# Second block, first mixer: where the forget gate's sums stand, and the head statistics

## The chip, the cores and the metric

The kernel runs on one core of one Trainium2 chip. The metric is the time of one launch on the device, in microseconds, smaller is better. The engines named are TensorE (matmuls), VectorE and ScalarE (which read its results out of PSUM, a memory of eight banks) and SyncE, which issues the weight transfers.

## The reference

The program computes two small networks one after the other on 256 tokens of width 1024, in float32. The first (attention, a pooling mixer, two mixtures of experts) ends with a norm; the second takes its result. The change lies in the second one's first mixer, `mixer_ab`, which has two branches: an mLSTM with four heads and an S5 state space model.

```
proj = x @ w_in;  xm, zm, us = the three thirds of proj
xc = silu(causal_dwconv(xm));  q, k from xc, v from xm (blocks of 4)
gates = concat(q, k, v) @ w_if + b_if            # per token: 4 input, 4 forget gates
b = cumsum(log_sigmoid(forget));  a = input - b;  m = running max of a
h = mLSTM(q, k, v) with weights exp(b_t - b_s + i_s - m_t), causal
hn = (h - mean(h)) * rsqrt(var(h) + EPS) * mh_gain      # per head and token
out_m = (hn + skip * xc) * silu(zm)
y = gelu(s5_ssm(us));  out_s = y * sigmoid(y @ w_glu + b_glu)
result = concat(out_m, out_s) @ w_out
```

The reference does the mLSTM in chunks of 64; the kernel does all 256 tokens at once, which needs the sums b and the running maximum m over the whole sequence before the heads' weights can be formed.

## The kernel before

Each stage of the program (`stage`, `run_stages`) hands one list of work to each engine, and no engine starts a stage before all have ended the one before. Within a stage every engine works through its own list strictly in the order written, and the lists meet at semaphores. The order around this change is therefore written by hand, in `all_pe`, `all_act` and `all_dve` of `mixer_ab`. `v(...)` makes VectorE wait for its own last instruction.

The pieces that the change touches:

- Tiles. TensorE's `project` (L1941) computes 128 output channels for all 256 tokens in eight matmuls (16 records in the trace). Tiles are numbered: US 0 to 3, XM 4 to 7, QKV 8 to 19, VT 20 and 21, GATES 22, and the gate branch's Z, 23 to 26. They rotate through banks 4, 5 and 6 of `ps`. ScalarE takes each tile out and counts `tile_taken`; `open_tile` waits for that count. The Z tiles are taken with Silu.
- The S5 branch runs in four pieces c. `states(c)` (L1951) makes the inputs of the state in banks 0 to 3; VectorE does `turn_in(c, 0..3)` (L2127), `turned_in(c)` (L2133, L2134), `scans(c)` (L2139, L2140, eight scans), `turn_out(c)` (L2146 to L2149); TensorE does `outputs(c)` (L1960) into bank 7, and VectorE `take_y(c)` (L2153). All pieces use the same buffers, so turn_in(c + 1) waits for outputs(c), and outputs(c) for turn_out(c).
- The forget gate. VectorE's `forget` (L2172 to L2175), two activations on ScalarE, VectorE's `log_forget` (L2179, counts `lf_ready`); TensorE's sums, three tiny matmuls with a triangle (L2038 to L2040, count `b_ready`); VectorE's `sums` (L2183, L2184, count `a_ready`); two transposes (L2043, `aT_ready`); VectorE's `running_max` (L2188 to L2191, `m_ready`); two transposes back (L2048, `mT_ready`); VectorE's `floor` (L2195). Before, the sums and the transposes of a come behind all four Z tiles, and use banks 4 and 5.
- The heads. `scores(h)` (L1971 to L1977), exponentials on ScalarE, `weigh(h)` (L2202), `mix(h)` (L1985 to L1987), `finish(h)` (L2210 to L2215), which writes `h_tok` and counts `num_taken`.
- The end. `skip` (L2240) makes skip * xc. `statistics` (L2222 bn_stats, L2226 bn_aggr, L2228 the variance plus EPS, `var_ready`); a square root on ScalarE; `normed` (L2232, L2235, `hn_ready`); eight transposes (L2066, `hnT_ready`); `mlstm_out` (L2246, L2248). Beside it the S5 branch: Gelu on ScalarE after the fourth take_y (L2105, `g_done`), TensorE's `glu(n)` (L1991), a sigmoid on ScalarE (L2110), `glu_out(n)` (L2252). ScalarE does Gelu first, then the square root, then the sigmoids.

Then the stage ends, and `project_out` (L1789) multiplies by w_out. Its weights are loaded while the mixer runs. The weights of the feed-forward behind it are asked for by SyncE when the stage has ended, because part of the weight ring serves as scratch space in this stage.

Of the kernel before, what the change touches and what calls it, by code (L numbers as in the profile page):

```python
# [20 lines left out]
P = 128  # L21
D = 1024
S = 256
TT = S // P
# [129 lines left out]
def build_program(nc, A, out):  # L154

    with ExitStack() as ctx:
# [1720 lines left out]
        def mixer_ab():  # L1877
# [50 lines left out]
            def bank(n):  # L1928

                return ps[:, 4 + n % 3, :]  # L1930

            def all_pe(pe):
                def open_tile(n):
                    if n >= 3:
                        pe.wait_ge(tile_taken, n - 2)
                    return bank(n)
# [90 lines left out]
                ins.then_inc(tile_ready, 1)  # L2027
                outputs(1)
                w = ring.take(pe, ("ab_in", 1))
                for j in range(4):  # L2030
                    project(w, j, Z + j)
                    if j == 1:
                        states(3)
                release(pe)

                pe.wait_ge(tile_taken, Z + 4)
                pe.wait_ge(lf_ready, 1)
                pe.matmul(ps[:, 4, 0:4], const("upto"), t1[:, 0, :], start=True, stop=True)  # L2038
                pe.matmul(ps[:, 4, 4:8], ones, t1[:, 0, :], start=True, stop=False)
                pe.matmul(ps[:, 4, 4:8], const("upto"), t1[:, 1, :], start=False, stop=True).then_inc(b_ready, 1)  # L2040
                pe.wait_ge(a_ready, 1)
                for t in range(TT):
                    ins = pe.transpose(ps[0:4, 5, t * P:(t + 1) * P], a_tok[:, t, :], ident)  # L2043
                ins.then_inc(aT_ready, 1)
                outputs(2)
# [3 lines left out]
                ins.then_inc(mT_ready, 1)  # L2049

                scores(0)
# [11 lines left out]
                pe.wait_ge(hn_ready, 8)  # L2063
                for h in range(4):
                    for t in range(TT):
                        ins = pe.transpose(ps[:, 4 + h // 2, (h % 2) * S + t * P:(h % 2) * S + (t + 1) * P], h_tok[:, t, h, :], ident)  # L2066
                ins.then_inc(hnT_ready, 1)
# [44 lines left out]
            def all_dve(dve):  # L2112
# [68 lines left out]
                def sums():  # L2181
                    dve.wait_ge(b_ready, 1)
                    v(dve.tensor_copy(b_tok, ps[:, 4, 0:8].rearrange("p (t h) -> p t h", t=TT)))  # L2183
                    dve.tensor_tensor(a_tok, pre[:, :, 0:4], b_tok, ALU.subtract).then_inc(a_ready, 1)  # L2184

                def running_max():
                    dve.wait_ge(aT_ready, 1)
                    v(dve.tensor_copy(a_rows[0:4, :], ps[0:4, 5, 0:S]))  # L2188
                    v(dve.tensor_tensor_scan(m_rows[0:4, :], ones[0:4, 0:1].to_broadcast([4, S]), a_rows[0:4, :], 0.0,
                                             ALU.mult, ALU.max))  # L2190
                    dve.tensor_scalar(m_rows[0:4, :], m_rows[0:4, :], -1.0, None, ALU.mult).then_inc(m_ready, 1)  # L2191
# [26 lines left out]
                def statistics():  # L2218
                    dve.wait_ge(num_taken, 4)
                    for t in range(TT):  # L2220
                        for h in range(4):
                            ins = dve.bn_stats(stats[:, t, h, :], h_tok[:, t, h, :])  # L2222
                    v(ins)
                    for t in range(TT):
                        for h in range(4):
                            ins = dve.bn_aggr(mean_var[:, t, h, :], stats[:, t, h, :])  # L2226
                    v(ins)
                    dve.tensor_scalar(sd, mean_var[:, :, :, 1], EPS, None, ALU.add).then_inc(var_ready, 1)  # L2228

                def normed():  # L2230
                    dve.wait_ge(sd_ready, 1)
                    v(dve.reciprocal(rstd, sd))  # L2232
                    for t in range(TT):
                        for h in range(4):
                            dve.tensor_scalar(h_tok[:, t, h, :], h_tok[:, t, h, :], mean_var[:, t, h, 0:1], rstd[:, t, h:h + 1],  # L2235
                                              ALU.subtract, ALU.mult).then_inc(hn_ready, 1)
# [6 lines left out]
                def mlstm_out():  # L2243
                    dve.wait_ge(hnT_ready, 1)
                    for h in range(4):
                        v(dve.scalar_tensor_tensor(out=conv[:, h, :], in0=ps[:, 4 + h // 2, (h % 2) * S:(h % 2 + 1) * S],  # L2246
                                                   scalar=col("ab_mh_gain_2", h), in1=conv[:, h, :], op0=ALU.mult, op1=ALU.add))
                        dve.tensor_tensor(mixT[:, h, :], conv[:, h, :], szT[:, h, :], ALU.mult)  # L2248
# [29 lines left out]
                forget()  # L2278
                take_y(1)
# [3 lines left out]
                turned_in(2)  # L2283
                scans(2, range(4))
                sums()
                turn_out(2)
                running_max()
                take_y(2)
                for i in range(4):
                    turn_in(3, i)  # L2290
                    if i == 0:
                        floor()
# [11 lines left out]
                skip()  # L2304
                finish(3)
                take_y(3)
                statistics()
# [381 lines left out]
```

## Time and profile before

| | |
|---|---|
| median of 3 runs | 2192.69 us (2184.86 to 2197.79) |
| the profiled execution, its own time | 2188.47 us |
| its span | 2186.4 us, 22473 instructions |
| TensorE matmul busy | 1731.5 us (79%) |
| VectorE busy | 501.8 us (23%) |
| ScalarE busy | 218.1 us (10%) |
| the mixer of this change | 1336 to 1454 us of the span |

The span is the profiled execution from its first to its last instruction; its own time holds what lies around the span, too. Times in the views are microseconds from the span's start. A timeline row has the start, the length, the engine, the line of the code, the operation with its output and inputs and the number of instructions merged in it, and in brackets how long the engine was idle before it and what ended that. Buffers carved out of one large tile are all called arena, hT, xn, gates or ring_buffer. PEclk is the granted clock of TensorE: 1.00 is 2.4 GHz, 0.50 is 1.2 GHz, and a value between them is a mean over the slice.

### The profile page before, as it was taken

Reading aid. Unit: us, or ns where it says so; the run is one execution under the profiler, and the core shown is the slowest. Engines: PE = TensorE matmul, PEld = TensorE weight load, DVE = VectorE, ACT = ScalarE, POOL = GpSimd, SP = SyncE. Lnnn points to the kernel's source line nnn. Section 1 sums busy time; section 2 is a strip of 40 time slices with the busy share of each in tenths; the row PEclk is TensorE's granted clock in tenths of the full one; section 3 lists DMA queues with packets and bytes.
Section 4 is the critical chain, followed back from the end, with each engine's and each line's share of the span. In section 5 each row is a group of like instructions: output and inputs, shape, how many; then the busy total and the mean of one; then the engine's idle time right before and its main releaser. Section 6 shows DMA issues by size and latency. Waiting matters only on the chain. (4 is left out here: it accounts for less than half of the span.)

```text
span 2186.4 us, 22473 instructions
## 1 busy us (share of the span) xinstructions
PE 1731.5 (79%) x9018; PEld 1000.1 (46%) x9019; DVE 501.8 (23%) x1168; ACT 218.1 (10%) x510; POOL 97.9 (4%) x125
## 2 busy tenths in 40 slices
PE   5999978866666576776666657878999899889998
PEld 3755553322222253232222215646885486558853
DVE  1213362111101125411111016861000203420001
ACT  1001020000000020000000001321000212110000
POOL 1010010000000007500000000000000000000000
PEclk9999968978877867898787778889999899899999
DMA  9969249999999956799999994133335434124330
GB/s 363 385 234 406 93 181 402 421 422 422 422 422 422 409 233 250 322 406 421 422 422 422 422 408 158 39 140 122 142 107 210 164 116 154 39 87 154 116 135 19
DMA packets 122665, 581.10 MB, mean 266 GB/s; under 512 B 10820, under 2 KB 15272, under 8 KB 67160
## 3 DMA queue, kind: packets, MB, share of 16 engines
q1 hardware_dynamic: 120416, 573.90, 65.4%
q0 software_dynamic: 1104, 2.86, 0.4%
q10 hardware_dynamic: 1064, 3.17, 0.4%
q8 instruction: 60, 0.98, 0.2%
q14 instruction: 21, 0.17, 0.0%
HBM read 578.86 MB, written 1.05 MB: 265 GB/s over the span
## 5 line engine op out<-in xcount | busy, mean ns | idle before, releaser
L1306 PE MATMUL ps<-ring_buffer,arena 128*32 128x512 f32 x2048 | 309.6, 763 | 170.6 <-DMA ring_buffer<-in_exp_w 167.9
L1831 PE MATMUL ps<-hT,ring_buffer 128*128 128x256 f32 x1408 | 309.9, 382 | 4.1 <-issue 2.6
L1831 PEld LDWEIGHTS ps<-hT,ring_buffer 128*128 128x128 f32 x1408 | 268.7, 192 | 45.2 <-issue 6.3
L1306 PEld LDWEIGHTS ps<-ring_buffer,arena 128*32 128x32 f32 x2048 | 82.1, 135 | 384.8 <-issue 325.0
L1331 PE MATMUL ps<-ring_buffer,arena 128*32 128x512 f32 x1088 | 155.8, 725 | 100.3 <-DMA ring_buffer<-in_exp_w 89.3
L1839 PE MATMUL ps<-ring_buffer,arena 128*128 128x512 f32 x352 | 154.2, 595 | 3.0 <-DVE arena L1872 1.9
L1331 PEld LDWEIGHTS ps<-ring_buffer,arena 128*32 128x32 f32 x1088 | 41.0, 130 | 204.3 <-issue 191.6
L1496 DVE TENSOR_TENSOR arena<-arena,ps 128x512 f32<-128x512 f32 x18 | 19.2, 1065 | 411.6 <-PE ps L1306 411.6
L1839 PEld LDWEIGHTS ps<-ring_buffer,arena 128*128 128x128 f32 x352 | 65.9, 190 | 90.4 <-issue 87.8
L1276 PE MATMUL ps<-arena,xn 128*128 128x128 f32 x640 | 82.0, 289 | 12.9 <-DVE arena L1466 12.9
L1276 PEld LDWEIGHTS ps<-arena,xn 128*128 128x128 f32 x640 | 78.6, 203 | 28.1 <-issue 22.3
L2364 PE MATMUL ps<-hT,ring_buffer 128*128 128x256 f32 x384 | 87.1, 389 | 1.9 <-issue 1.0
L1872 DVE TENSOR_TENSOR arena<-arena,ps 128x256 f32<-128x256 f32 x44 | 18.5, 421 | 295.9 <-ACT arena L1866 295.9
L2364 PEld LDWEIGHTS ps<-hT,ring_buffer 128*128 128x128 f32 x384 | 74.4, 195 | 15.0 <-issue 3.5
L1419 ACT ACTIVATE arena<-ps,mod,gain 128x128 f32<-128x128 f32 x72 | 27.1, 457 | 419.0 <-PE ps L1276 419.0
L1789 PE MATMUL ps<-ring_buffer,hT 128*128 128x512 f32 x128 | 59.7, 627 | 3.3 <-DVEq L237 3.0
L715 PE MATMUL ps<-hT,ring_buffer 128*128 128x256 f32 x256 | 58.6, 391 | 3.2 <-ACTq L237 2.5
L1512 DVE TENSOR_TENSOR arena<-ps,gates 128x512 f32<-128x512 f32 x16 | 11.1, 692 | 211.8 <-PE ps L1331 211.8
L1345 PE MATMUL ps<-arena 128*128 128x512 f32 x128 | 59.3, 605 | 0.0
L499 PE MATMUL ps<-ring_buffer,arena 128*32 128x512 f32 x384 | 50.0, 642 | 9.2 <-DMA ring_buffer<-in_ada_w 8.3
L715 PEld LDWEIGHTS ps<-hT,ring_buffer 128*128 128x128 f32 x256 | 50.0, 197 | 13.0 <-issue 3.4
L1436 ACT ACTIVATE arena<-ps 128x512 f32<-128x512 f32 x18 | 10.8, 597 | 416.7 <-PE ps L1306 416.7
(501 smaller groups left out, 1565.5 us busy)
## 6 DMA issues: line engine op xcount, KB each, us to landing
ring_buffer<-in_exp_w SPq DMA_DIRECT2D x384, 1024.0 KB, 18.6
ring_buffer<-in_ffn_w SPq DMA_DIRECT2D x30, 2048.0 KB, 7.9
ring_buffer<-in_ada_w SPq DMA_DIRECT2D x24, 2048.0 KB, 12.6
ring_buffer<-in_c_w_in SPq DMA_DIRECT2D x8, 2048.0 KB, 7.8
ring_buffer<-in_attn_w_in SPq DMA_DIRECT2D x6, 2048.0 KB, 17.0
ring_buffer<-in_ab_w_in SPq DMA_DIRECT2D x3, 2048.0 KB, 19.8
ring_buffer<-in_ffn_w SPq DMA_DIRECT2D x6, 1024.0 KB, 7.8
ring_buffer<-in_attn_w_o SPq DMA_DIRECT2D x2, 2048.0 KB, 12.8
```

The source lines that it names most:

```text
L499: pe.matmul(ps[g * WIDE:(g + 1) * WIDE, COND, :], spread_c[:, 2 * pair + k, row:row + WIDE], w[:, k, 512 * n:512 * (n + 1)], start=(first ...
L715: ins = pe.matmul(ps[:, n % BANKS, 0:S], w[:, k, j * P:(j + 1) * P], hT[:, k, :], start=(k == 0), stop=(k == KD - 1))
L1276: ins = pe.matmul(ps[:, BXA + k // 4, (k % 4) * P:(k % 4 + 1) * P], xn[:, t, k * P:(k + 1) * P], pick[:, t, :], start=(t == 0), stop=(t == ...
L1306: ins = pe.matmul(ps[c, bank, :], tokens[:, 4 * phase + k, c], halves[j][:, k, :], start=(phase == 0 and k == 0), stop=(phase == 1 and k = ...
L1331: ins = pe.matmul(ps[c, bank, :], tokens[:, 2 * phase + k, c], halves[j][:, k, half * 512:(half + 1) * 512], start=(phase == 0 and k == 0) ...
L1345: ins = pe.matmul(ps[:, 2 * half + t, :], weights[:, t, :], values[:, half * 512:(half + 1) * 512], start=opens, stop=False, skip_group_ch ...
L1419: return eng.activation(o, src, ACT.Identity, scale=G[:, k:k + 1], bias=H[:, k:k + 1])
L1496: dve.tensor_tensor(to.rearrange("c (h k p) -> c h p k", h=2, k=2), gated.rearrange("c (h p k) -> c h p k", h=2, k=2), ps[:, bank, :].rear ...
L1789: ins = pe.matmul(ps[:, 2 * c + t, :], fT[:, k, t * P:(t + 1) * P], w[:, k, :], start=(k == 0), stop=(k == KD - 1))
L1831: ins = pe.matmul(ps[:, f % 8, i * S:(i + 1) * S], w[:, k, j * P:(j + 1) * P], hT[:, k, :], start=(k == 0), stop=(k == KD - 1))
L1839: ins = pe.matmul(ps[:, 2 * half + t, :], aT[:, r + k, t * P:(t + 1) * P], w[:, k, 512 * half:512 * half + 512], start=(r + k == 0), stop= ...
L2364: ins = pe.matmul(ps[:, n % 8, 0:S], w[:, k, j * P:(j + 1) * P], hT[:, k, :], start=(k == 0), stop=(k == KD - 1))
```

## The change

The sums, the transposes of a and of m all use bank 6, and the Z tiles rotate through banks 4 and 5 only. TensorE's order becomes: gates, Z0, outputs(1), Z1, the sums, Z2, the transposes of a, states(3), Z3, the transposes of m, outputs(2), scores. In VectorE's list sums moves ahead of scans(2), running_max ahead of turn_out(2), floor ahead of take_y(2), and skip ahead of take_y(1). The statistics are done for one head at a time: those of heads 0 to 2 between finish(2) and finish(3), that of head 3 and the variance (now `variances`) between finish(3) and take_y(3). `normed` goes head by head, the transposes of two heads are signalled as soon as they are done, and mlstm_out waits for each half. The number of computing instructions stays the same.

```diff
             def bank(n):
-                return ps[:, 4 + n % 3, :]
+
+                return ps[:, 4 + n % 3, :] if n < Z else ps[:, 4 + (n - Z) % 2, :]
             def all_pe(pe):
                 def open_tile(n):
-                    if n >= 3:
+                    if n >= Z:
+                        pe.wait_ge(tile_taken, n - 1)
+                    elif n >= 3:
                         pe.wait_ge(tile_taken, n - 2)
                     return bank(n)
@@ -2025,29 +2028,29 @@
                         ins = pe.matmul(o[:, 8 * t:8 * t + 8], qkvT[:, n, t * P:(t + 1) * P], w_if[:, n, :],
                                         start=(n == 0), stop=(n == 11))
                 ins.then_inc(tile_ready, 1)
+                w = ring.take(pe, ("ab_in", 1))
+                project(w, 0, Z)
                 outputs(1)
-                w = ring.take(pe, ("ab_in", 1))
-                for j in range(4):
-                    project(w, j, Z + j)
-                    if j == 1:
-                        states(3)
-                release(pe)
-
-                pe.wait_ge(tile_taken, Z + 4)
+                project(w, 1, Z + 1)
                 pe.wait_ge(lf_ready, 1)
-                pe.matmul(ps[:, 4, 0:4], const("upto"), t1[:, 0, :], start=True, stop=True)
-                pe.matmul(ps[:, 4, 4:8], ones, t1[:, 0, :], start=True, stop=False)
-                pe.matmul(ps[:, 4, 4:8], const("upto"), t1[:, 1, :], start=False, stop=True).then_inc(b_ready, 1)
+                pe.matmul(ps[:, 6, 0:4], const("upto"), t1[:, 0, :], start=True, stop=True)
+                pe.matmul(ps[:, 6, 4:8], ones, t1[:, 0, :], start=True, stop=False)
+                pe.matmul(ps[:, 6, 4:8], const("upto"), t1[:, 1, :], start=False, stop=True).then_inc(b_ready, 1)
+                project(w, 2, Z + 2)
                 pe.wait_ge(a_ready, 1)
                 for t in range(TT):
-                    ins = pe.transpose(ps[0:4, 5, t * P:(t + 1) * P], a_tok[:, t, :], ident)
+                    ins = pe.transpose(ps[0:4, 6, t * P:(t + 1) * P], a_tok[:, t, :], ident)
                 ins.then_inc(aT_ready, 1)
-                outputs(2)
+                states(3)
+                project(w, 3, Z + 3)
+                release(pe)
                 pe.wait_ge(m_ready, 1)
                 for t in range(TT):
                     ins = pe.transpose(ps[:, 6, t * P:(t + 1) * P], m_rows[:, t * P:(t + 1) * P], ident)
                 ins.then_inc(mT_ready, 1)
-
+                outputs(2)
+
+                pe.wait_ge(tile_taken, Z + 4)
                 scores(0)
                 for h in range(4):
                     if h < 3:
@@ -2060,11 +2063,12 @@
                 pe.wait_ge(g_done, 1)
                 for n in range(3):
                     glu(n, w)
-                pe.wait_ge(hn_ready, 8)
                 for h in range(4):
+                    pe.wait_ge(hn_ready, 2 * h + 2)
                     for t in range(TT):
                         ins = pe.transpose(ps[:, 4 + h // 2, (h % 2) * S + t * P:(h % 2) * S + (t + 1) * P], h_tok[:, t, h, :], ident)
-                ins.then_inc(hnT_ready, 1)
+                    if h % 2:
+                        ins.then_inc(hnT_ready, 1)
                 glu(3, w)
                 release(pe)
@@ -2180,12 +2184,12 @@
                 def sums():
                     dve.wait_ge(b_ready, 1)
-                    v(dve.tensor_copy(b_tok, ps[:, 4, 0:8].rearrange("p (t h) -> p t h", t=TT)))
+                    v(dve.tensor_copy(b_tok, ps[:, 6, 0:8].rearrange("p (t h) -> p t h", t=TT)))
                     dve.tensor_tensor(a_tok, pre[:, :, 0:4], b_tok, ALU.subtract).then_inc(a_ready, 1)
                 def running_max():
                     dve.wait_ge(aT_ready, 1)
-                    v(dve.tensor_copy(a_rows[0:4, :], ps[0:4, 5, 0:S]))
+                    v(dve.tensor_copy(a_rows[0:4, :], ps[0:4, 6, 0:S]))
                     v(dve.tensor_tensor_scan(m_rows[0:4, :], ones[0:4, 0:1].to_broadcast([4, S]), a_rows[0:4, :], 0.0,
                                              ALU.mult, ALU.max))
                     dve.tensor_scalar(m_rows[0:4, :], m_rows[0:4, :], -1.0, None, ALU.mult).then_inc(m_ready, 1)
@@ -2215,23 +2219,23 @@
                         ins = dve.tensor_scalar(h_tok[:, t, h, :], o[:, t, 0:M_DIM], r[:, t:t + 1], None, ALU.mult)
                     ins.then_inc(num_taken, 1)
-                def statistics():
-                    dve.wait_ge(num_taken, 4)
+                def statistics(h):
+                    dve.wait_ge(num_taken, h + 1)
                     for t in range(TT):
-                        for h in range(4):
-                            ins = dve.bn_stats(stats[:, t, h, :], h_tok[:, t, h, :])
+                        ins = dve.bn_stats(stats[:, t, h, :], h_tok[:, t, h, :])
                     v(ins)
                     for t in range(TT):
-                        for h in range(4):
-                            ins = dve.bn_aggr(mean_var[:, t, h, :], stats[:, t, h, :])
+                        ins = dve.bn_aggr(mean_var[:, t, h, :], stats[:, t, h, :])
                     v(ins)
+
+                def variances():
                     dve.tensor_scalar(sd, mean_var[:, :, :, 1], EPS, None, ALU.add).then_inc(var_ready, 1)
                 def normed():
                     dve.wait_ge(sd_ready, 1)
                     v(dve.reciprocal(rstd, sd))
-                    for t in range(TT):
-                        for h in range(4):
+                    for h in range(4):
+                        for t in range(TT):
                             dve.tensor_scalar(h_tok[:, t, h, :], h_tok[:, t, h, :], mean_var[:, t, h, 0:1], rstd[:, t, h:h + 1],
                                               ALU.subtract, ALU.mult).then_inc(hn_ready, 1)
@@ -2241,8 +2245,8 @@
                     v(ins)
                 def mlstm_out():
-                    dve.wait_ge(hnT_ready, 1)
                     for h in range(4):
+                        dve.wait_ge(hnT_ready, h // 2 + 1)
                         v(dve.scalar_tensor_tensor(out=conv[:, h, :], in0=ps[:, 4 + h // 2, (h % 2) * S:(h % 2 + 1) * S],
                                                    scalar=col("ab_mh_gain_2", h), in1=conv[:, h, :], op0=ALU.mult, op1=ALU.add))
                         dve.tensor_tensor(mixT[:, h, :], conv[:, h, :], szT[:, h, :], ALU.mult)
@@ -2276,20 +2280,20 @@
                 scans(1, range(4))
                 turn_out(1)
                 forget()
+                skip()
                 take_y(1)
                 log_forget()
                 for i in range(4):
                     turn_in(2, i)
                 turned_in(2)
+                sums()
                 scans(2, range(4))
-                sums()
+                running_max()
                 turn_out(2)
-                running_max()
+                floor()
                 take_y(2)
                 for i in range(4):
                     turn_in(3, i)
-                    if i == 0:
-                        floor()
                 turned_in(3)
                 weigh(0)
                 scans(3, range(2))
@@ -2301,10 +2305,12 @@
                 turn_out(3)
                 weigh(3)
                 finish(2)
-                skip()
+                for h in range(3):
+                    statistics(h)
                 finish(3)
+                statistics(3)
+                variances()
                 take_y(3)
-                statistics()
                 normed()
                 for n in range(3):
                     glu_out(n)
```

## Rows read from the trace of the kernel before

**Rows 1.** Busy time by stretch: stretch, length, then each engine's busy time (instructions).
```profile
core 0: us, PE busy (x) PEld busy (x) DVE busy (x) ACT busy (x) POOL busy (x), PEclk, DMA share, GB/s
1336.00:1454.00 118.00, 96.46 (x596) 77.21 (x594) 96.61 (x180) 29.35 (x55) 0.00 (x0) 0.90 0.11 41
```

**Rows 2.** Waits of VectorE, 1336 to 1455: total, times, longest.
```profile
DVE xn L2153 <- PE ps L1960: 6.0, 3, 2.8
DVE arena L2183 <- PE ps L2040: 4.3, 1, 4.3
```

**Rows 3.** Timeline of TensorE at the mixer's end.
```profile
1438.07 0.80 PE L1985 MATMUL ps<-arena,hT 128*128 128x129 f32 x2 [5.50 <-DVE hT L2202]
...
1444.29 5.42 PE L1991 MATMUL ps<-xn,ring_buffer 128*128 128x256 f32 x24 [1.79 <-ACT xn L2105]
...
1454.55 29.80 PE L1789 MATMUL ps<-ring_buffer,hT 128*128 128x512 f32 x64 [2.24 <-DVEq L237]
```

**Rows 4.** Timeline of TensorE, 1368 to 1413.
```profile
1368.16 1.07 PE L1960 MATMUL ps<-ring_buffer,arena 128*32 128x256 f32 x16
...
1369.48 0.62 PE L1960 MATMUL ps<-gates,arena 128*32 128x256 f32 x8
...
1387.52 1.93 PE L1960 MATMUL ps<-ring_buffer,arena 128*32 128x256 f32 x16 [0.32 <-DVE gates L2149]
...
1390.75 7.17 PE L1941 MATMUL ps<-hT,ring_buffer 128*128 128x256 f32 x32
...
1412.62 1.93 PE L1960 MATMUL ps<-ring_buffer,arena 128*32 128x256 f32 x16 [4.28 <-DVE gates L2149]
```

**Rows 5.** Timeline of VectorE, 1390 to 1417.
```profile
1390.97 0.48 DVE L2153 SCALAR_TENSOR_TENSOR xn<-arena,cols,ps 128x256 f32<-128x256 f32 x1 [2.84 <-PE ps L1960]
...
1391.44 2.35 DVE L2127 TENSOR_TENSOR ring_buffer<-ps,arena 128x1024 f32<-128x1024 f32 x2
...
1407.54 0.17 DVE L2183 COPY arena<-ps 128x8 f32<-128x8 f32 x1 [4.29 <-PE ps L2040]
...
1407.82 1.22 DVE L2146 TENSOR_TENSOR ring_buffer<-xn,arena 128x1024 f32<-128x1024 f32 x1
...
1412.49 0.41 DVE L2188 COPY ring_buffer<-ps 4x256 f32<-4x256 f32 x1
...
1416.34 0.48 DVE L2153 SCALAR_TENSOR_TENSOR xn<-arena,cols,ps 128x256 f32<-128x256 f32 x1 [2.42 <-PE ps L1960]
```

**Rows 6.** Granted clock of TensorE in slices of 1 us.
```profile
1390.00:1391.00 1.00, 1.00 (x13) 0.83 0.00 0
1410.00:1411.00 1.00, 0.00 (x0) 0.91 0.00 0
1434.00:1435.00 1.00, 0.00 (x0) 0.86 0.00 0
1441.00:1442.00 1.00, 1.00 (x20) 0.73 0.02 8
```

**Rows 7.** Timeline of VectorE at the mixer's end.
```profile
1439.24 1.13 DVE L2240 TENSOR_SCALAR arena<-arena,cols 128x256 f32<-128x256 f32 x4
1440.41 0.16 DVE L2210 COPY small<-ps 128x2 f32<-128x2 f32 x1
...
1442.57 0.48 DVE L2153 SCALAR_TENSOR_TENSOR xn<-arena,cols,ps 128x256 f32<-128x256 f32 x1 [0.77 <-PE ps L1960]
1442.97 1.64 DVE L2222 BATCH_NORM_STATS2 arena<-ring_buffer 128x6 f32<-128x128 f32 x8
1444.64 0.64 DVE L2226 BATCH_NORM_AGGREGATE arena<-arena 128x2 f32<-128x6 f32 x8
...
1445.77 0.20 DVE L2232 RECIPROCAL arena<-arena 128x8 f32<-128x8 f32 x1 [0.28 <-ACT arena L2107]
```

**Rows 8.** Groups by line, VectorE: count, busy us, mean ns of one, idle before.
```profile
L2222 DVE BATCH_NORM_STATS2 arena<-ring_buffer 128x6 f32<-128x128 f32 x8 | 1.6, 278 | 0.0
```

**Rows 9.** Timeline of ScalarE: Gelu.
```profile
1443.09 1.06 ACT L2105 ACTIVATE xn<-xn 128x1024 f32<-128x1024 f32 x1 [10.93 <-DVE xn L2153]
```

## The prediction

> **What bounds the kernel now.** I read the busy time by stretches first. The kernel takes 2186.4 us of span, but the changed lines all lie in one stretch of 118 us, in which VectorE is busy for 96.61 us and TensorE for 96.46 [rows 1]. Busy shares don't say which of two equally busy engines leads, so the waits of VectorE in that stretch come next: 4.3 us once at the forget gate's sums (L2183), and 6.0 us in three pieces at take_y (L2153) [rows 2]. The timelines give the order. Between these waits VectorE is gapless to the last instruction of the stage, while TensorE waits for it again and again: 4.28 us ahead of outputs(2), 5.50 ahead of mix(3) [rows 3, 4]. The stage ends when VectorE does, and the output projection (L1789) starts 2.24 us after TensorE's last work, released by VectorE's queue [rows 3]. So the price of this change is what it does to VectorE's chain between 1387 and 1454 us. The stages before are untouched. The stages after have their weights long before they need them: the output projection begins at once when released, and the weight stream of the feed-forward starts only when the whole stage is done. They are shifted and nothing else.
>
> **Edit A: one gate tile (Z0) before outputs(1).** In the kernel before, outputs(1) starts on TensorE at 1387.52, 0.32 us behind the gates' matmuls (done at 1387.2), and ends at 1390.75, 3.23 us; take_y(1) runs on VectorE at 1390.97 after 2.84 us idle [rows 4, 5]. Now project(Z0) stands ahead of it in the same queue. Two projections take 7.17 us at the full clock, one 3.58 [rows 4]. But here the granted clock is at its lower level, 1.2 GHz, until about 1390.5 (the slice 1390:1391 shows 0.83, the mean of both levels) [rows 6]. So 3.3 us of Z0 pass at half speed and do 1.65 us of its work, and 1.93 follow at full speed: Z0 ends at 1392.45. outputs(1) then runs at the full clock, as outputs(0) did: 1368.16 to 1369.48 + 0.62, that is 1.94 us [rows 4]. It ends at 1394.4, and take_y(1) starts at 1394.55, which is 3.6 us later than before. Nothing else can be done by VectorE in that time except skip() (1440.41 - 1439.24 = 1.17 us [rows 7]), which is moved into this gap and so costs nothing here. Bounds: 1.9 us if the clock is full from the start of Z0, 7.0 if it is low throughout (7.17 + 3.3). I take 3.6, the value at the clock of these rows.
>
> **Edit B: sums and maximum between the tiles, in bank 6.** The sums' matmuls no longer stand behind the fourth Z tile, but behind the second: Z1 ends at 1394.4 + 3.58 = 1398.0, the forget gate's logarithm comes right behind take_y(1) (1395.0), so this added wait holds nothing, and b is ready at about 1398.8. VectorE wants it after turn_in(2) and turned_in(2), at 1402.1: no wait. The 4.29 us of idle before L2183 go [rows 2, 5]. On TensorE Z2 (to 1402.4), the transposes of a, states(3) (eight small products, about 1 us) and Z3 follow, to 1407.7. The wait for a holds Z3 by 0.1 us; states(3) is about 5 us later than before, but turn_in(3) wants it at 1417 only. What is late next: running_max now stands ahead of turn_out(2) instead of behind it. Before, its 1.43 us (1412.49 to 1413.92) lay in the time in which VectorE waited for outputs(2); now they are on the chain [rows 5]. From take_y(1) to take_y(2) the chain is now: take_y and log_forget 0.47, turn_in(2) to the last scan(2) 11.81 (1391.44 to 1407.54 - 4.29), sums 0.28, running_max 1.43, turn_out(2) 4.67 (1407.82 to 1412.49), and outputs(2) with its handovers 3.85 (1412.49 to 1416.34, TensorE again at the lower level after 4 us of waiting) [rows 4, 5]. That is 22.51 against 25.37 before: 2.9 us gained. With edit A's 3.6 take_y(2) comes 0.7 us later than before; floor(), taken out of turn_in(3), returns 0.07. So VectorE is 0.6 us late when turn_in(3) is done, and up to finish(2) nothing in that part is reordered, on either engine; TensorE's scores and mixes follow VectorE there, and move with it.
> Bounds for B: a gain of 4.3 us if running_max were hidden after all, and of 1.5 if outputs(2) were delayed by its place behind the maximum's transposes.
>
> **Edit C: statistics head by head, skip() away.** Before, finish(2) was done at 1439.24, then skip() 1.17, finish(3) from 1440.41 to 1441.80, 0.77 us of waiting for outputs(3), and take_y(3) at 1442.57 [rows 7]. Now three statistics stand between, and the fourth and variances() ahead of take_y(3). All eight bn_stats took 1.64 us in a row, 0.205 each, but one alone lasts 0.278; all eight bn_aggr took 0.64 [rows 7, 8]. Head by head each pair is closed by a wait for its own end: 0.205 + 0.278 + 0.03 for two bn_stats, 0.23 + 0.04 for two bn_aggr, together 0.8 us a head, 3.2 for four against 2.35 in one piece. So: 1439.24 + 0.6 (late) + 2.4 + 1.4 (finish(3)) + 0.8 + 0.25 (a wait for finish(3), variances) = 1444.7 for take_y(3), against 1442.57: 2.1 us later. What was behind take_y(3) on VectorE is now ahead of it, but take_y(3) leads the longer branch: Gelu on ScalarE follows it at once (1443.09), and the square root, whose result VectorE takes at 1445.77, stands behind Gelu and a table load in ScalarE's own queue [rows 7, 9]. The reciprocal therefore comes 3.1 to 3.2 us behind take_y(3) either way, and statistics that were free inside these microseconds are now paid.
> The Trainium skill, "VectorE: DVE Perf Modes", section on the drain, has it that eight copies take the same time with a semaphore after each as with one at the end. By it the four heads would cost 2.35 us and take_y(3) would come 0.85 us earlier. The row of 0.205 each against 0.278 alone speaks for my value, since these overlap when nothing is waited for [rows 7, 8].
>
> **The tail.** glu(0) to glu(2) start when Gelu is done and took 5.42 us at the full clock [rows 3]. mlstm_out waits behind glu_out(2), so for these; that the head transposes signal in two halves gives nothing, since the first half is done only when glu_out(2) is anyway. But TensorE has now been idle for longer before glu: outputs(3) ends 0.6 us later, Gelu 2.1 later, so the gap of 1.79 us becomes 3.3 [rows 3]. After the work that ended at 1408.3 (4.28 us before outputs(2)) the clock fell within the slice 1410:1411, 2.6 us later; after 1432.6 (5.50 us before mix(3)) within 1434:1435 [rows 6]. Once work is back it takes about 3.4 us at the lower level (mix(3) at 1438.07 to slice 1441:1442) [rows 6]. So glu runs for about 3.3 us at half speed, which costs 1.65.
> The Trainium skill, "TensorE: Matmul & The Clock Gate", section "What's actually happening", says that the clock follows how busy the engine has been lately; by that rule a longer gap speaks against this change. The trace agrees in its two falls.
> Bounds for this term: 0 (the gap of 1.79 us left the clock at its upper level) and 2.7 (all of glu at half speed until it is half as long again).
>
> **Sum.** +3.6 - 2.9 - 0.1 + 1.5 + 1.65 = +3.7 us. The profiled execution took 2188.47 us, so 2192.2 by it. That execution is 4.2 us under the median of the runs shown, 2192.69; against the median it is 2196.4, which I take as 2196.
>
> **Rivals.**
> 1. *The clock doesn't bite.* Z0 runs at full speed from its start (-1.7), the gap before glu leaves the clock up (-1.65), and the split statistics cost what they did in one piece (-0.85): -0.5 us, 2192. For it: the gap of 1.79 us stayed at the upper level. Against: at the place of Z0 the trace shows the lower level for certain.
> 2. *The idle times really come out of the chain.* 4.3 us before the sums, 0.8 before take_y(3) and skip's 1.2 go, and only running_max's 1.4 is paid: -4.9, 2188. For it: these are the waits of VectorE that the profile shows. It needs outputs(1) not to be later, and TensorE's queue is in order, so there is little for it.
> 3. *The other side: TensorE becomes the bound while it turns the Z tiles.* If the clock stays at its lower level from 1387 us on, each of the four tiles takes 7.17 us instead of 3.58. Z0 to Z3, outputs(1), states(3) and the small products then last some 36 us and outputs(2) ends 11 us later than before; with the 3 us of the last part that is +14, 2207. It decides from the point where Z3 ends after turn_out(2), 1413 us. Against it: before, the clock was up again 3.3 us after work came, and the new order has TensorE busier there.
> 4. *Nothing that a chain shows*: the change is in effect neutral (+-2 us), as errors of my terms cancel.
>
> **Chances.** The forecast (+2 to +6) 55%; rivals 1 and 4 together 27%; rival 2 10%; rival 3 3%; 5% for what I don't see. All but rival 3 are below the 0.5%, 11 us, that a measurement of this kernel can tell from no change: its three runs lie 13 us apart. That spread, more than the mechanisms, sets the range: 2187 (rival 2, near the lowest run) to 2204. Faster by over 0.5%: 3%. Within: 92%. Slower: 5%.
>
> **What would show it.** In the trace after: take_y(1) 3 to 4 us later than 1390.97 (a wait of about 5 us before it, with skip ahead of it); no wait before the copy of the sums; take_y(2) within a microsecond of 1416.3; statistics of a head 0.8 us; take_y(3) near 1444.7; the granted clock at 0.5 when glu begins; the output projection starting near 1458 instead of 1454.55. I am wrong if take_y(1) is not late, if VectorE waits anywhere between take_y(1) and turn_out(2), or if the output projection starts before 1454.

## The result, and the profile after

The changed kernel takes 2192.23 us (median of 20 runs, 2178.86 to 2205.87). With 17 more runs beside it, the kernel before has a median of 2180.27 over 20 runs; its first three alone, known ahead, had 2192.69. The ratio is 1.0048, interval 1.0028 to 1.0067: slower by about 10.5 us (the two medians are 12.0 us apart), just inside the 0.5% that the prediction counts as no change. The prediction had 2196 us and +3.7. Of all runs of the experiments below, one, of the fourth, took 5801.83 us, where the eleven others of its kernel took 2169 to 2190 us; it is left out of the ratio.

The page of the changed kernel, its own time 2191.72 us, has the same amount of work (two instructions more in the record); the last row is the granted clock in tenths, in 40 slices of the span:

```profile
span 2189.9 us, 22475 instructions
PE 1729.5 (79%) x9018; PEld 1001.6 (46%) x9019; DVE 501.7 (23%) x1168; ACT 218.2 (10%) x510; POOL 98.0 (4%) x125
...
PEclk9999988978887778988887888889999899599999
```

**In the mixer** the chain went as predicted. The absolute times are about 9.8 us earlier than those of the kernel before, because the untouched stages ahead of the mixer were shorter in this execution; so intervals are compared. VectorE's timeline answers to [rows 5, 7], with L2157 for take_y, L2244 skip, L2187 the copy of the sums, L2192 running_max, L2225 bn_stats:

```profile
1378.26 1.14 DVE L2244 TENSOR_SCALAR arena<-arena,cols 128x256 f32<-128x256 f32 x4
1384.57 0.48 DVE L2157 SCALAR_TENSOR_TENSOR xn<-arena,cols,ps 128x256 f32<-128x256 f32 x1 [5.17 <-PE ps L1963]
...
1392.09 0.17 DVE L2187 COPY arena<-ps 128x8 f32<-128x8 f32 x1
...
1397.16 0.41 DVE L2192 COPY ring_buffer<-ps 4x256 f32<-4x256 f32 x1
...
1407.03 0.48 DVE L2157 SCALAR_TENSOR_TENSOR xn<-arena,cols,ps 128x256 f32<-128x256 f32 x1 [3.69 <-PE ps L1963]
...
1429.85 0.47 DVE L2225 BATCH_NORM_STATS2 arena<-ring_buffer 128x6 f32<-128x128 f32 x2
1430.36 0.25 DVE L2228 BATCH_NORM_AGGREGATE arena<-arena 128x2 f32<-128x6 f32 x2
1430.64 0.49 DVE L2225 BATCH_NORM_STATS2 arena<-ring_buffer 128x6 f32<-128x128 f32 x2
...
1434.74 0.47 DVE L2157 SCALAR_TENSOR_TENSOR xn<-arena,cols,ps 128x256 f32<-128x256 f32 x1
...
1437.85 0.20 DVE L2236 RECIPROCAL arena<-arena 128x8 f32<-128x8 f32 x1 [2.64 <-ACT arena L2111]
```

The copy of the sums has no wait any more (4.29 us before), skip lies in front of the wait of 5.17 us for outputs(1), and nothing stands idle before the last take_y. Each head's statistics take 0.79 us. TensorE's timeline answers to [rows 3, 4]; L1944 is project, L1963 outputs, L1994 glu:

```profile
1377.11 5.46 PE L1944 MATMUL ps<-hT,ring_buffer 128*128 128x256 f32 x16
1382.50 1.07 PE L1963 MATMUL ps<-ring_buffer,arena 128*32 128x256 f32 x16
...
1436.44 8.22 PE L1994 MATMUL ps<-xn,ring_buffer 128*128 128x256 f32 x24 [3.47 <-ACT xn L2109]
...
1449.48 0.70 PE L1789 MATMUL ps<-ring_buffer,hT 128*128 128x512 f32 x1 [2.21 <-DVEq L237]
```

Z0 took 5.46 us, since it began at the lower clock; glu(0) to glu(2) took 8.22 us instead of 5.42. The granted clock in slices of 1 us shows why: the gap before glu is now 3.47 us long and the clock falls in it.

```profile
1435.00:1436.00 1.00, 0.00 (x0) 0.65 0.00 0
1436.00:1437.00 1.00, 0.56 (x1) 0.50 0.00 0
...
1441.00:1442.00 1.00, 1.00 (x4) 0.50 0.00 0
1442.00:1443.00 1.00, 1.00 (x6) 0.94 0.00 0
```

**Behind the mixer** is what the prediction did not have: the heads of the second mixer, `mixer_c`, whose code and inputs are untouched. Before, these 192 matmul records took 39.0 us from their first to the next output projection, now 50.6. Slices of 5 us from the start of the heads, in the kernel before:

```profile
1862.61:1867.61 5.00, 3.75 (x29) 1.00 0.91 345
1867.61:1872.61 5.00, 5.00 (x24) 0.56 0.00 0
1872.61:1877.61 5.00, 5.00 (x31) 0.76 0.00 0
1877.61:1882.61 5.00, 4.97 (x37) 1.00 0.00 0
```

and in the changed one:

```profile
1856.24:1861.24 5.00, 3.75 (x29) 1.00 0.88 336
1861.24:1866.24 5.00, 5.00 (x24) 0.57 0.02 3
1866.24:1871.24 5.00, 5.00 (x23) 0.50 0.00 0
1871.24:1876.24 5.00, 5.00 (x22) 0.50 0.00 0
...
1891.24:1896.24 5.00, 5.00 (x20) 0.50 0.00 0
```

In both the clock falls between 5.5 and 6 us into the heads. Before, it rises again 12.4 us in; now it stays at 1.2 GHz to the end, and TensorE does 20 to 24 records in 5 us instead of 37. On the page of the changed kernel it is the one digit 5 in the row PEclk, the 35th of 40 slices.

So the spans differ like this: mixer from outputs(0) to the output projection +4.7; the output projection behind it -1.7 (29.8 to 28.1 us, since the clock no longer falls in it); the feed-forward between +0.4; the heads +11.6; the output projection behind these -2.1 (30.15 to 28.1, since it now starts at the upper clock); what follows +0.4; and what lies ahead of outputs(0) -9.8. Sum +3.5, which is 2189.9 - 2186.4. Without the last term the two executions are 13.3 us apart, which lies inside the interval of the ratio (6 to 15 us). That term is no effect of the change: over all executions traced below the mixer begins between 1322.7 and 1341.6 us, with the same code ahead of it.

### The profile page after: what moved, and what is told of

The parts are those of the page before. It is cut to its first block and busy times, and to the rows that moved or that the text cites. A ratio compares the mean times of both kernels' runs of the same rounds, so it can differ in the third digit from the quotient of the medians.

```text
span 2189.9 us, 22475 instructions
## 1 busy us (share of the span) xinstructions
PE 1729.5 (79%) x9018; PEld 1001.6 (46%) x9019; DVE 501.7 (23%) x1168; ACT 218.2 (10%) x510; POOL 98.0 (4%) x125
## 5 line engine op out<-in xcount | busy, mean ns | idle before, releaser
L1306 PE MATMUL ps<-ring_buffer,arena 128*32 128x512 f32 x2048 | 305.0, 753 | 172.3 <-DMA ring_buffer<-in_exp_w 169.6
L1331 PE MATMUL ps<-ring_buffer,arena 128*32 128x512 f32 x1088 | 155.5, 724 | 102.4 <-DMA ring_buffer<-in_exp_w 92.2
L1276 PEld LDWEIGHTS ps<-arena,xn 128*128 128x128 f32 x640 | 79.2, 205 | 27.2 <-issue 21.5
L499 PE MATMUL ps<-ring_buffer,arena 128*32 128x512 f32 x384 | 49.3, 633 | 9.0 <-DMA ring_buffer<-in_ada_w 8.1
```

Source lines behind the costliest of these rows:

```text
L499: pe.matmul(ps[g * WIDE:(g + 1) * WIDE, COND, :], spread_c[:, 2 * pair + k, row:row + WIDE], w[:, k, 512 * n:512 * (n + 1)], start=(first ...
L1276: ins = pe.matmul(ps[:, BXA + k // 4, (k % 4) * P:(k % 4 + 1) * P], xn[:, t, k * P:(k + 1) * P], pick[:, t, :], start=(t == 0), stop=(t == ...
L1306: ins = pe.matmul(ps[c, bank, :], tokens[:, 4 * phase + k, c], halves[j][:, k, :], start=(phase == 0 and k == 0), stop=(phase == 1 and k = ...
L1331: ins = pe.matmul(ps[c, bank, :], tokens[:, 2 * phase + k, c], halves[j][:, k, half * 512:(half + 1) * 512], start=(phase == 0 and k == 0) ...
```

## Experiments

All times in us. "Mixer" runs from outputs(0) to the output projection, "heads" from the first matmul of mixer_c's heads to its output projection, each from the one profiled execution; the ratio is that of the timed runs to the kernel before. (The first expectations measure the mixer from its first project. Those first tiles passed at the lower clock in some executions, 33.2 to 33.4 us to outputs(0) instead of 31.1, ahead of everything that was changed; so I compare from outputs(0).)

| kernel | to take_y(1) | to take_y(2) | to take_y(3) | glu to projection | mixer | heads | ratio (95%) |
|---|---|---|---|---|---|---|---|
| before | 22.8 | 25.4 | 26.2 | 10.3 | 86.4 | 39.0 | 1 |
| changed | 26.2 | 22.5 | 27.7 | 13.0 | 91.1 | 50.6 | 1.0048 (1.0028-1.0067) |
| 1 outputs(1) first | 23.0 | 21.5 | 27.7 | 11.8 | 85.7 | 41.4 | 1.0041 (1.0020-1.0061) |
| 2 statistics whole | 26.2 | 22.5 | 26.1 | 10.2 | 86.7 | 39.0 | 1.0010 (0.9987-1.0033) |
| 3 both undone | 22.8 | 21.6 | 26.4 | 10.2 | 82.8 | 39.0 | 0.9981 (0.9962-1.0000) |
| 4 and maximum late | 22.8 | 19.5 | 27.0 | 10.2 | 81.3 | 39.0 | 0.9990 (0.9965-1.0016) |
| 5 before again | 22.8 | 25.4 | 26.3 | 10.3 | 86.4 | 39.0 | 1.0000 (0.9981-1.0019) |
| 6 only the split | 22.8 | 25.4 | 27.6 | 13.3 | 90.8 | 50.5 | 1.0067 (1.0040-1.0094) |
| 7 before, heads filled | 22.9 | 25.4 | 26.3 | 10.3 | 86.5 | 36.2 | 0.9983 (0.9964-1.0002) |
| 8 changed, heads filled | 26.2 | 22.5 | 27.7 | 13.0 | 91.1 | 36.2 | 1.0002 (0.9982-1.0021) |
| 9 changed, glu filled | 26.2 | 22.5 | 27.7 | 10.2 | 88.3 | 39.0 | 1.0000 (0.9975-1.0026) |
| 10 before, shifted | 22.8 | 25.4 | 26.2 | 14.1 | 90.2 | 41.4 | 1.0026 (1.0004-1.0047) |
| 11 changed again | 26.2 | 22.5 | 27.7 | 13.1 | 91.1 | 50.6 | 1.0036 (1.0008-1.0064) |
| 12 as 4, heads filled | 22.8 | 19.5 | 27.0 | 10.2 | 81.3 | 36.2 | 0.9955 (0.9934-0.9976) |

**Experiments 1 to 4: the parts of the change.**

```diff
 # 1
+                outputs(1)
                 project(w, 0, Z)
-                outputs(1)
 # 2: statistics() in one piece as before
-                for h in range(3):
-                    statistics(h)
                 finish(3)
-                statistics(3)
-                variances()
                 take_y(3)
+                statistics()
+                variances()
 # 3: 1 and 2;  # 4: 3, and
-                running_max()
                 turn_out(2)
-                floor()
+                running_max()
 # with floor() in turn_in(3), and outputs(2) ahead of the transposes of m
```

> The changed kernel with outputs(1) ahead of project(Z0) again; all else as changed. Measured in the trace by the mixer's length (first project of the mixer to the first matmul of the output projection: 117.5 us before, 122.2 changed). Theory 1 (the added us in the mixer are VectorE's chain, 3.4 of them by the gate tile ahead of outputs(1)): take_y(1) comes 3.4 us earlier, nothing new is waited for, mixer 118.8, or 117.5 if outputs(2), which then waits for a shorter time, keeps the full clock. Rival (TensorE's order does not matter, the clock sets it): mixer stays within 1 us of 122.2. For the whole program two theories on the other 7 us that the 20 timed runs show beyond the mixer: theory D (a draw: the heads of mixer_c, 38 us at 2.4 GHz and 50 at 1.2, fall into either by chance, whatever this change does): totals of this kernel lie in two groups some 10 us apart, as those of before and changed do, with its share of slow ones anywhere. Theory P (the change shifts mixer_c against something, which makes its heads slow): this kernel, 3 us shorter, has a share of slow ones different from the changed one and no one kernel has both in plenty.

> The changed kernel with the statistics in one piece behind take_y(3), as before; skip stays early, Z0 stays ahead of outputs(1). Theory 1 (the split puts the statistics ahead of take_y(3), and by it Gelu, the square root and glu, which then starts at the lower clock): take_y(3) 1.5 us earlier than changed, the wait before glu back at 1.8 us, glu(0) to glu(2) 5.4 us instead of 8.2, mixer 122.2 - 1.5 - 2.8 = 117.9 us. If glu's lower clock had nothing to do with the gap: 120.7. Rival (the statistics are hidden either way): 122.2. Theory D or P for the whole as in the first run.

> Both undone: of the change only the sums and the maximum between the tiles in bank 6, and skip in the wait for outputs(1). Theory 1: 2.9 us of the idle before the sums are gained and nothing is paid, mixer 114.5 us, against 117.5 before; ratio to before 0.9987 by the chain alone. Rival (the terms do not add, TensorE becomes the bound): mixer 116 or more. Theory D: the total may still lie up to 7 us off that on either side, by the share of slow runs.

> As the third, and running_max behind turn_out(2) again, with outputs(2) ahead of the maximum's transposes: the maximum lies in VectorE's wait for outputs(2). Theory 1: another 1.4 us, and outputs(2) waits for 1 us instead of 4, so it keeps the full clock and is 1.3 us shorter: mixer 111.8 to 113.1 us. Rival: the transposes of the maximum, now behind outputs(2), delay scores(0) and weigh(0): mixer 114.5 or more.

In the mixer theory 1 holds in all four, with larger gains than expected in the first and the third. Putting outputs(1) first brings 5.4 us: 3.2 at take_y(1), 1.0 because outputs(2) begins after a shorter wait and partly at the upper clock, 1.2 in glu. Leaving the statistics whole brings 4.4: 1.6 at take_y(3) and 2.8 in glu. Of the third kernel's 3.6 us gain, 3.7 lie between take_y(1) and take_y(2). The fourth gains 2.1 more there and gives 0.7 back by take_y(3). VectorE's waits at take_y(2) and take_y(3) in the fourth kernel:

```profile
1402.78 0.48 DVE L2157 SCALAR_TENSOR_TENSOR xn<-arena,cols,ps 128x256 f32<-128x256 f32 x1 [0.70 <-PE ps L1963]
...
1429.80 0.48 DVE L2157 SCALAR_TENSOR_TENSOR xn<-arena,cols,ps 128x256 f32<-128x256 f32 x1 [2.21 <-PE ps L1963]
```

The totals tell something else: the first kernel, whose mixer is 0.7 us shorter than before, is 9 us slower. The two slow kernels, 1 and the changed one, are those with split statistics, and they have the longer heads. (The first kernel's profiled execution, 2180.14 us, was one of its fastest; its median is 2187.5. So its 41.4 us may understate what its heads take as a rule; one profiled execution can't tell.)

**Experiments 5 and 6: is the slow head stage a draw?** The fifth is the kernel before; the sixth has of the change only the split and the place of skip.

```diff
 # 6, against the kernel before
                 forget()
+                skip()
 ...
                 finish(2)
-                skip()
+                for h in range(3):
+                    statistics(h)
                 finish(3)
-                take_y(3)
-                statistics()
+                statistics(3)
+                variances()
+                take_y(3)
```

> The kernel before, unchanged. From outputs(0) to the output projection its trace showed 86.4 us (changed: 91.1), and the heads of mixer_c 39.0 us (changed: 50.6 and, in the first experiment, 41.4; all kernels without the split statistics 39.0). Theory D (the heads' clock is a draw): its total comes within 0.3% of the other runs of before, and its heads are 39 or 50. Theory S (the split statistics make glu start at the lower clock, and that shifts what the clock does further on): heads 39.0 again.

> The kernel before with only the statistics head by head and skip in the wait for outputs(1). In the mixer take_y(3) comes 1 to 1.5 us later and glu(0) to glu(2) run 1.6 to 2.8 us longer at the lower clock: outputs(0) to the output projection 89.0 to 90.7 us. Theory D: total 2.6 to 4.3 us above before (0.12 to 0.2%), up to 5 us off that by the draw. Theory S: total 9 to 13 us above before (0.4 to 0.6%), as the first experiment (which had the split too, and +0.41% with a mixer 0.7 us shorter than before), and heads above 39.0.

The fifth fits both theories. The sixth speaks for S: +0.67% for a mixer that is 4.4 us longer (about 14.6 us in all), with heads of 50.5 us. The figure lies a little above S's 0.4 to 0.6%, which its interval from 0.40 to 0.94% holds; D had 0.2% and up to 5 us (0.23%) more, which reaches just into that interval. glu in it, after a gap of 3.16 us:

```profile
1435.29 8.46 PE L1991 MATMUL ps<-xn,ring_buffer 128*128 128x256 f32 x24 [3.16 <-ACT xn L2105]
```

**Experiments 7 and 8: do the heads hold the missing time?** Products that nobody reads fill two waits of TensorE.

```diff
 # behind mixer_c's last projection
+                wait_bank(pe, n)
+                for k in range(6):
+                    pe.matmul(ps[:, n % 8, 0:S], hT[:, k, 0:P], hT[:, k, :], start=True, stop=True)
 # in the heads
                 update(0)
+                for k in range(2):
+                    pe.matmul(ps[:, 7, 0:S], hT[:, k, 0:P], hT[:, k, :], start=True, stop=True)
```

> The kernel before with eight products that nobody reads (leading to no output): six behind the last projection of mixer_c, in the 2.7 us in which TensorE waits for the stage to end, and two in the 1.2 us wait behind the first update. If the heads' clock falls because of these two waits, the granted clock stays at its upper level through the heads, and these take 36 to 37 us instead of 39.0 (at a cost of 0.5 us for what is not hidden): total 2 us below before where the heads are at 39, and 11 to 14 below in executions in which they were at 50. Rival: the clock falls whatever stands in the waits, heads 39 or 50.

> The changed kernel with the same fill. Both theories put the 6 us that the change costs beyond the mixer into the heads of mixer_c. If that is so and the fill works, this kernel lies only 4.7 us (0.2%) above the filled kernel before. If it stays 10 us above it, the 6 us lie elsewhere.

The seventh kernel's heads, from their start, run wholly at the upper clock:

```profile
1853.46:1858.46 5.00, 4.82 (x33) 1.00 0.85 322
1858.46:1863.46 5.00, 4.97 (x39) 1.00 0.00 0
1863.46:1868.46 5.00, 4.98 (x37) 1.00 0.00 0
```

Filled, before and changed both have heads of 36.2 us, and their ratios differ by 0.0019, 4.1 us: that fits the mixer's 4.7, though each ratio is known to some 4 us only. With the 11.6 us of the traces this puts the rest of the slowdown into the heads. The fill alone makes the changed kernel equal to the kernel before, within its interval.

**Experiments 9 to 11: what makes the heads slow?**

```diff
 # 9, against the changed kernel
                 outputs(3)
+                for k in range(7):
+                    pe.matmul(ps[:, 4, 0:S], qkvT[:, k, 0:P], qkvT[:, k, :], start=True, stop=True)
 # 10, against the kernel before
                 glu_out(3)
+                for _ in range(12):
+                    v(dve.tensor_scalar(conv[:, 0, :], conv[:, 0, :], 1.0, None, ALU.mult))
```

> The changed kernel with seven products that nobody reads, behind outputs(3), in the 3.5 us in which TensorE waits for Gelu. glu should keep the upper clock: outputs(0) to the output projection 91.1 - 2.8 = 88.3 us. Theory S1 (it is glu's lower clock, not the 1.4 us of shift, that decides what the clock does in the heads of mixer_c): heads 39.0, total 2 to 3 us (0.1%) above before. Theory S2 (the shift decides): heads 50, total 8 to 9 us (0.4%) above before.

> The kernel before with twelve small VectorE instructions at the end of the mixer, about 4 us that change no number. TensorE waits that much longer for the output projection. Theory S2: heads 50, total 13 to 16 us above before (0.6 to 0.7%). Theory S1: heads 39.0, total 4 to 6 us above (0.2 to 0.3%), the output projection starting at the lower clock.

> The changed kernel, unchanged. If the long heads belong to it: heads near 50 again (41 at least), total 0.4 to 0.6% above before. If they were a draw: heads 39.0, and a total within 0.3% of before.

The eleventh repeats the long heads and the slower total (+0.36%, a little under the expected 0.4). In the ninth glu keeps the upper clock behind a fill of 3.29 us:

```profile
1438.05 3.29 PE L2063 MATMUL ps<-ring_buffer 128*128 128x256 f32 x14
1441.58 5.42 PE L1994 MATMUL ps<-xn,ring_buffer 128*128 128x256 f32 x24 [0.24 <-ACT xn L2111]
```

Its VectorE chain up to take_y(3) is that of the changed kernel to 0.01 us, yet the heads are at 39.0 and the total at that of before. That speaks for theory S1 and against S2. The tenth is between: no low clock in glu(0) to glu(2), a wait of 6.07 us before the output projection, and heads in which the clock falls after 1.2 us already and rises for good 15 us in:

```profile
1865.93:1870.93 5.00, 3.76 (x24) 0.62 0.91 346
1870.93:1875.93 5.00, 5.00 (x22) 0.50 0.00 0
1875.93:1880.93 5.00, 5.00 (x24) 0.52 0.01 3
1880.93:1885.93 5.00, 4.99 (x38) 1.00 0.00 0
```

Its total of +0.26% is what S1 expected, its 41.4 us are not. So the low clock in glu is not the only thing that can move the clock's course in the heads: here a longer wait, behind which the output projection began at the lower clock, went with another course.

Without the fill of the heads three courses were seen: down and up again (39.0, six executions, none with a longer glu), down and not up (50.6, three, all with glu(0) to glu(2) longer by 2.8 us or more), and down early (41.4, two: the first experiment, whose glu is 1.6 us longer, and the tenth). By which way something 400 us earlier picks one of them was not measured and stays open. A draw would seldom sort them so, but it is not ruled out by eleven executions. Nor is it shown that a kernel takes the same course in every execution. The two kernels with two traces each, before and changed, repeated theirs; the other kernels have one trace, and the spread of the timed runs (2176 to 2206 us for the changed kernel) can't tell, since the start of the mixer alone varies by 19 us.

**Experiment 12: the parts that pay.**

> The fourth experiment's kernel (sums and maximum in the waits, outputs(1) first, statistics whole) with the fill of the heads of the seventh. outputs(0) to the output projection 81.3 us, heads 36.2: 5.1 + 2.8 us below before in one execution, so a total 0.3 to 0.5% below before.

The mixer and the heads came out as expected, and the total is 0.45% below before, about 10 us: the lowest ratio of all these kernels, with an interval wholly below 1. Against the third, fourth and seventh, which hold parts of it, the intervals overlap.

## Why the prediction was right, and where it was wrong

- The path: the prediction called VectorE gapless between its waits up to the end of the stage. It was not: in the trace before it also waited 0.28 us at the reciprocal [rows 7] and 1.30 us for a sigmoid behind glu, as the row below shows. So the chain's end runs over TensorE, as the prediction's own term for the tail has it.

```profile
1450.25 0.43 DVE L2252 TENSOR_TENSOR hT<-xn,hT 128x256 f32<-128x256 f32 x1 [1.30 <-ACT hT L2110]
```

- Edit A: take_y(1) was forecast 3.6 us late and was 3.4 late. Experiment 1 takes 3.2 of it out again.
- Edit B: 22.51 us from take_y(1) to take_y(2) forecast, 22.46 measured. Experiments 3 and 4 show the other side of it: without edit A outputs(2) begins after a shorter wait, at a higher clock, so the sums' gain was 3.7 us, and 5.9 with the maximum put back behind turn_out(2).
- Edit C: take_y(3) forecast 2.1 us late, and it was 2.0 (3.4 - 2.9 + 1.5). 0.79 us a head against 0.8. The value from the step of 0.205 us between two bn_stats in a row and the 0.278 us that one record lasts was right. The Trainium skill ("VectorE: DVE Perf Modes", "The DRAIN you can't avoid") has eight copies take the same time with a semaphore after each as with one behind the last. For these short instructions the trace does not agree: four times 0.79 is 3.2 us, against 2.35 in one piece.
- The tail: that glu would begin at the lower clock was right; the term was mis-sized, 2.8 us instead of 1.65. I had taken the low stretch from mix(3) and outputs(3), 3.4 us, but in glu it lasted from 1436.4 to 1442.1, 5.7 us. That is nearly all of the difference between +4.7 and +3.7 for the mixer.
- The step that failed is in the first paragraph: "They are shifted and nothing else", of the stages after. I had looked only at their weights, and not at where TensorE's clock moves in them. The heads of mixer_c are a stage in which one course of the clock costs 11.6 us more than another, three times the whole sum; the prediction had this at nothing. Rival 3 had the low clock as a price, but put it into the Z tiles, where the clock rose 3.6 us after Z0's start.
- The range and "within 0.5%" held, the second narrowly. But the time of 2196 came near the measured 2192.23 partly by luck: it stood on a median of three runs that was 12 us above that of all 20. The effect was about three times the forecast one.

## What to carry to other kernels

A wait of TensorE can have a price beyond its own length: where the granted clock fell in it, the work behind ran at 1.2 GHz for some microseconds (glu: 8.22 us instead of 5.42), and in this kernel that went with another course of the clock in a later stage. Before moving work on another engine ahead of a hand-over to TensorE, look at how long TensorE will stand idle; and look in the trace for later stages in which the granted clock falls and rises again, for there it may take another course. Products that nobody reads, put into such a wait, took 0.46% and 0.48% off the changed kernel here (experiments 8 and 9), where undoing its two costly parts took off 0.67% (experiment 3); each of these ratios is known to about 0.2%.

Work that hides in an engine's wait at one place is paid in full when it is moved ahead of the instruction that starts the next chain: here statistics and take_y.

## What the runs showed of the hardware

The same 192 matmul records, with the same code ahead of them from the mixer's end on, took 39.0, 41.4 or 50.6 us, each length repeated to 0.1 us in other executions, and 36.2 with the fill. The courses differ in where the clock falls against the work, as slices of 1 us show: 5.6 us behind the heads' start in all six executions with 39.0 us, 5.7 to 5.8 in all three with 50.6, and 1.2 in both with 41.4. The slices with the fall, for the kernel before (heads from 1862.61), the changed one (1856.24) and experiments 6 (1855.50) and 10 (1865.93):

```profile
1868.00:1869.00 1.00, 1.00 (x8) 0.61 0.00 0
1861.00:1862.00 1.00, 1.00 (x9) 0.98 0.00 0
1861.00:1862.00 1.00, 1.00 (x9) 0.64 0.00 0
1867.00:1868.00 1.00, 1.00 (x7) 0.55 1.05 406
```

Why 0.1 us should decide whether the clock comes back, if it is that which decides, no run here shows.

In the changed kernel TensorE was busy in every microsecond of the heads at 1.2 GHz for 35 us and the clock did not rise, whereas in the mixer it rose 3.6 us after Z0's start and 5.7 us after glu's. The Trainium skill, "TensorE: Matmul & The Clock Gate", "What's actually happening", has the clock follow how busy the engine has been; the busy times shown here do not tell the heads from glu, so no run here shows what makes the difference.

That the output projection runs at the upper clock throughout in one kernel, and has a fall early in it in another, after nearly the same wait (2.21 and 2.24 us: 28.1 and 29.8 us for the same 64 records), was not expected either.
